# A second modulation's multiply-adds placed in other quanta of one fp32 kernel

## The reference, cut to what matters

```python
for l in range(2):
    mod  = silu(c)     @ w_mod[l] + b_mod[l]       # 2048 -> 6144: shift, scale, gate
    cmod = silu(c_ctx) @ w_mod[l] + b_mod[l]
    h  = rmsnorm(x,  norm_g[l]) * (1 + scale)  + shift
    hc = rmsnorm(cx, norm_g[l]) * (1 + cscale) + cshift
    ...                                            # u = h @ w_in; attention mixers; y * silu(gate part)
    x  = x  + gate  * (y  @ w_o[l])
    cx = cx + cgate * (yc @ w_o[l])                # only l = 0
```

## Time and profile before

| | us |
|---|---|
| median of 3 runs | 2377.14 (2376.76 to 2377.52) |
| the profiled execution, device time | 2377.5 |
| its span in the trace | 2375.7 |
| PE busy | 2330.6 |
| DVE busy | 1502.2 |
| ACT busy | 1040.7 |
| POOL busy | 271.1 |

### The profile page before, as it was taken

One profiled execution on the slowest core, in us unless ns is written; L12 is line 12 of the kernel. 1 busy time (PEld: TensorE's weight loads), 2 busy tenths in 40 slices (PEclk: granted clock), 3 DMA queues, 4 the chain that ended last, 5 costly groups with the idle time before them and its releaser, 6 DMA issues. The chain is left out here.

```text
span 2375.7 us, 31312 instructions
## 1 busy us (share of the span) xinstructions
PE 2330.6 (98%) x11556; PEld 1895.8 (80%) x11556; DVE 1502.2 (63%) x2508; ACT 1040.7 (44%) x1755; POOL 271.1 (11%) x403
## 2 busy tenths in 40 slices
PE   6999999999999999999999999999999999999998
PEld 1578888877778888877878889878888888998887
DVE  2288555666777887877656666675675544544655
ACT  3232333344443222524544455444454445654543
POOL 0011120111110000012121000100110001101200
PEclk9999999999999999999999999999999999999999
DMA  9978454544434756585665556765655676667653
GB/s 369 365 265 282 163 168 138 167 153 160 143 113 166 238 190 224 181 270 190 191 199 156 164 190 202 223 214 162 218 173 187 191 224 196 203 196 239 190 194 135
DMA packets 236423, 474.60 MB, mean 200 GB/s; under 512 B 18886, under 2 KB 47924, under 8 KB 235504
## 3 DMA queue, kind: packets, MB, share of 16 engines
q1 hardware_dynamic: 210768, 394.27, 51.0%
q0 software_dynamic: 25216, 77.81, 10.4%
q10 hardware_dynamic: 288, 0.52, 0.1%
HBM read 438.59 MB, written 33.94 MB: 199 GB/s over the span
## 5 line engine op out<-in xcount | busy, mean ns | idle before, releaser
L2334 PE MATMUL pp<-w_hi,hT_hi 128*128 128x512 f32 (+4 forms) x2520 | 1004.1, 398 | 1.8 <-DVE w_lo L1682 1.8
L2336 PE MATMUL pp<-w_hi,hT_lo 128*128 128x512 f32 (+4 forms) x2520 | 964.9, 383 | 0.0
L1682 DVE TENSOR_TENSOR w_lo<-raw,w_hi 128x1024 fp32r<-128x1024 f32 (+4 forms) x562 | 658.6, 1176 | 481.0 <-ACT w_hi L1379 479.4
L2335 PE MATMUL pp<-w_lo,hT_hi 128*128 128x512 f32 (+4 forms) x2520 | 962.1, 382 | 0.0
L1379 ACT ACTIVATE w_hi<-raw 128x1024 fp32r<-128x1024 f32 (+4 forms) x562 | 569.4, 1018 | 427.3 <-PE pp L2336 300.8
L2334 PEld LDWEIGHTS pp<-w_hi,hT_hi 128*128 128x128 f32 x2520 | 473.9, 188 | 100.5 <-issue 21.4
L2336 PEld LDWEIGHTS pp<-w_hi,hT_lo 128*128 128x128 f32 x2520 | 473.0, 188 | 89.5
L2335 PEld LDWEIGHTS pp<-w_lo,hT_hi 128*128 128x128 f32 x2520 | 474.5, 188 | 80.4 <-issue 4.3
L1792 DVE SCALAR_TENSOR_TENSOR arena<-raw,cT,arena 128x512 f32<-128x512 f32 x240 | 170.4, 745 | 2.1 <-DMA raw<-in_w_mod_dram 0.2
L1549 ACT ACTIVATE arena<-pY 128x512 f32<-128x512 f32 (+2 forms) x122 | 63.5, 520 | 197.9 <-PE pY L2504 192.6
L2329 PE MATMUL pp<-hT_hi,w_hi 128*128 128x512 f32 x352 | 149.6, 425 | 0.0
(11 more groups left out here) (358 smaller groups left out, 2010.7 us busy)
## 6 DMA issues: line engine op xcount, KB each, us to landing
raw<-in_w_in_dram SPq DMA_DIRECT2D x168, 512.0 KB, 4.2
raw<-in_w_mod_dram SPq DMA_DIRECT2D x153, 512.0 KB, 5.4
raw<-in_e_w_in_dram SPq DMA_DIRECT2D x90, 512.0 KB, 5.5
raw<-in_w_o_dram SPq DMA_DIRECT2D x64, 512.0 KB, 4.2
raw<-in_o_w_in_dram SPq DMA_DIRECT2D x64, 512.0 KB, 4.7
raw<-in_w_out_dram SPq DMA_DIRECT2D x64, 512.0 KB, 3.9
raw<-in_w_in_dram SPq DMA_DIRECT2D x56, 440.0 KB, 4.0
arena<-in_w_mod_dram SPq DMA_DIRECT2D x39, 512.0 KB, 11.2
```

The costliest lines, as they stand in the source:

```text
L1682: dve.tensor_tensor(w_lo[:, g.s % SPLIT, 0:n], raw_of(g)[:, 0:n], w_hi[:, g.s % SPLIT, 0:n].bitcast(F32), ALU.subtract).then_inc(lo_done, 1)
L2334: pe.matmul(dst, hT_hi[:, kk, o:o + P], hi[:, k, :], start=a, stop=False)
L2335: pe.matmul(dst, hT_hi[:, kk, o:o + P], lo[:, k, :], start=False, stop=False)
L2336: ins = pe.matmul(dst, hT_lo[:, kk, o:o + P], hi[:, k, :], start=False, stop=z)
```

## The change

Only `Work.room` is edited.

```diff
         if slot < a0:
-            return (slot - b0) % 4 in (0, 2)
+            return (slot - b0) % 4 in (0, 2, 3)
         if slot < C["y0_3"].q0:
-            return (slot - a0) % 4 in (0, 3)
+            p = (slot - C["y0_0"].q0) % 32
+            if slot > C["y0_0"].q0 + 16 and p in (0, 3, 31):
+                return 0
+            return (slot - a0) % 4 in (0, 3) or slot > C["y0_0"].q0 and p in (10, 14, 18)
```

## The result

| | before | after |
|---|---|---|
| median of 6 runs each | 2376.95 us (2375.42 to 2377.59) | 2392.99 us (2391.29 to 2399.15) |
| ratio | | 1.0072, 95% interval 1.0061 to 1.0082 |
| the profiled execution, span | 2377.5, 2375.7 | 2396.15, 2394.3 |
| granted TensorE clock over the span | 0.999 | 0.995 |

The kernel became slower by 16.0 us, outside the range of the forecast (2372.5 to 2386). The profiled execution stands 3.2 us above its median. The spans differ by 18.6 us, and that is what the traces are asked to explain.

A forecast was written before the change was run, and what follows sets the result against it. PE, busy 98% of the span, was taken as the bound, so only its idle time could be gained. -5.39 + 0.9 + 6.5 + 0.5 = +2.5 us gave 2380.0, as a median 2379.6; range 2372.5 to 2386.

The forecast's parts named there:

- (a): Ends of y0_0 and y0_1: PE's idle 0.89 and 1.55 us go; gain 2.44 us.
- (b): scale1_2's second fold waits for the first's reduction; folds move to 468 and 469; gain 0.34 us.
- (c): Head of the c heads: multiply-adds at 668 to 680 go and d_q's loads go out earlier; gain 2.08 us.
- (d): gate1_3's fold waits for bank O; at 660 no head uses the bank; gain 0.53 us.
- The first heads: Three quanta of four there: 33 more multiply-adds on DVE fit its idle time; cost nothing.
- C: Rival: DVE's cover in the first heads is used up, eight units lose about 0.7 each: +5.6, 2385 us; chance 0.06.
- D: Rival: the c heads' chain is one of latencies, so 2.08 of gain goes: 2381.7 us; chance 0.10.
- Quantum 468: Quanta 468 and 469: scale1_2's first fold stands just ahead of y_turn's transpose in bank O; cost 0.9 us (0.5 to 2.5).
- The largest term: Quanta 600 to 624: gate1_1's pair 5 holds its buffer over the gap, loads come late, PE stands 6.5 us (0 to 8).
- rival A: The stall at 624 does not come because buffers come free early enough: 2373.1 us; chance 0.20.
- Rival B: The ring does not recover; longer stall, store chain and 468 cost, or a second ACT wait: about 2386 us; chance 0.14.
- The store chain: c_kv's store and load: fuller queue plus 1.2, POOL's root without the multiply-add minus 0.7; net cost 0.5 us.

The follow-up runs named there:

- hold: The kernel after with all four gate1 chunks back at their places of before (first multiply-add at 597): 2374.97 us.
- straddle: The kernel before with gate1_0 one quantum sooner (596, was 597), so its pair 3 has multiply-adds at 600 and 612: 2393.24 us.
- first: The kernel before with only the first heads' line changed to three quanta in four, so gate1 starts at 581: 2396.43 us.
- keys: The kernel after with one more wait on SP: c_q1's pair 7 is loaded only when the first c head's keys are back: 2389.43 us.
- thin: The kernel after with the loads of gate1_0's and gate1_1's weight pairs cut to 8 of 512 columns: 2387.21 us.
- no600: The kernel after with no multiply-add beside quantum 600, so gate1_1's pair 5 lies wholly behind the gap (612 and 613): 2377.26 us.
- nokeys: The kernel after with gate1_1 from 612, gate1_3 from 684 and scale1_2 from 425, without an added SP wait for the keys: 2371.29 us.
- hold1: The kernel after with only gate1_1 held until quantum 612, gate1_0 staying at 581 to 592: 2374.62 us.

## Why the prediction was wrong

**The gains were right.** -5.39 was forecast. The traces show -2.6 for (a) and -0.85 for (b), for which 2.44 and 0.34 stood. For (c) and (d) 2.61 stood, and PE's idle time at 672 to 720 fell from 3.38 to 0.77, by just that. The quanta there are 4.5 faster because the folds of 676 and 719 went out of them too, some 0.6 each; they were not gained but stand at 644 and 660 now. The first heads cost nothing, as reasoned from the earlier trace rows; hold shows it in the time. Rivals C and D fall.

**Quantum 468:** 0.79 of idle time for the 0.9 forecast, 1.25 in the quanta's times.

**The largest term, 6.5 beside 624:** 6.58. The place, the start of it (one buffer held from 600 to 612), SP's gap and ACT's third wait came as written, and rival A falls. That the length agrees so closely is in part luck, for the chain before it ran otherwise. The term was one stall where the mechanism gives several. The first of ACT's waits, for a load that took 6.8 us and not 3.95, already holds an x_turn activation (2.43); the second holds gate1_1's last multiply-adds and so its fold (1.16). I had followed the chain to the one wait that ended last and not priced those before it. The quanta 608 to 656 cost 12.0 for 6.5.

**The step that failed** is the sentence "Once PE has stood, all other engines are ahead and no further stall follows." They are not ahead: PE stood because ACT and SP were late, and SP's lateness was in the ring, where each load waits for a side pair and each side pair for a load. At 1058.72, 43 us behind the stall, ACT still waited 7.73 us for a load. So quanta 656 to 672 cost 6.95 where the sum had 0.5. Of the kernels with the pair across the gap straddle pays 4.9 there, first 3.7, keys 3.0 and thin 2.8; no600, without it, pays 1.9. That a stall follows is shown; its size in after is not explained. Rival B had this in its condition (a second ACT wait) and stopped at 2386 with 0.14; it was the nearest to the truth, and still 7 us short.

That sentence is one of three parts of the error. The spans moved by 18.6 us for a forecast of 2.5, 16.1 too much: 6.5 at 656 to 672, 5.5 at 608 to 656 (above), 6.1 at 592 to 608, which had no term (below), and 0.35 at 468, less 2.6 by which the gains and the folds that moved away came to more.

**The store chain, 0.5 (0 to 3):** 4.59 of stall for 1.30, and 3.0 of slow clock. I had asked whether the queue would be fuller, and not whether ACT would bring the evictions late. keys shows the queue's share; no600, whose store waits 7.99 us and whose stalls there are 0.73 and 1.61, suggests that the state of the ring comes first. The minus 0.7 for POOL's root was wrong as well. It still takes 1.93 us, and the low half alone stands beside it (kernel after, POOL and DVE):

```profile
1083.78 1.93 POOL L1303 TENSOR_TENSOR stat<-stat 128x4 f32<-128x4 f32 x1 [5.60 <-DVE stat L1972]
```
```profile
1083.60 1.22 DVE L1685 TENSOR_TENSOR w_lo<-raw,w_hi 128x1024 fp32r<-128x1024 f32 x1
```

I had put the longer root down to the multiply-add, which was gone here. The two roots that I compared also have different shapes, 128x4 and 128x2. Compared at one shape, POOL's root still differs with what DVE does beside it: 128x2 took 0.71 us in the kernel before at 1068.26, where DVE started a low half 0.4 us into it, and 1.59 in nokeys at 1062.11, where one ran beside two thirds of it.

The Trainium skill (DMA: Bandwidth & Descriptors, Queues, rings and completion order) says that a DMA engine goes round between the queues that have work. The traces agree: POOL stood 9.77 us beside the row of loads and 6.00 with a load held.

**A place not looked at:** quanta 581 to 608. The table of the change has gate1_0 at 581 to 592 and gate1_1 from 593, at up to two multiply-adds per quantum, and the working begins at 600. Their loads share the ring and the DMA engines with out0_3's last pairs, just where the norm's chain begins, which x_turn needs at once. 6.1 us, 2.9 of it slow clock. The forecast had no term for them.

**The clock.** A stall was priced at its length. Three of them brought 7.6 us more.

As terms, from the earlier trace rows on: stalls 3.21 + 2.43 + 1.16 + 6.58 + 0.76 + 3.83 - 1.30 = 16.7; slow clock 7.6; 468 1.25; gate1_3's fold, now at 660, 0.6; and -2.6, -0.85 and -4.5. The sum is 18.2 for the 18.6 measured.

## What to carry to other kernels

When work is moved through a ring of buffers, look first for an item whose uses lie on both sides of a gap: its buffer holds the queue for the whole gap (25 us here). Moving the pair's first multiply-add to the other side, with those behind it one place on, was worth 16 us. After such a hold don't close the account at the first stall: follow the ring until it is again a lap ahead, price each wait of the in-order engine on the way, and add to every stall what the clock takes behind it. And walk through every stretch where the new table has work and the old had none, not only those where a rule changes.

## What the hardware showed that I had not expected

- PE idle of 3.21, 6.58 and 3.83 us (after) was each followed or overlapped by 6.8 us at 1.2 GHz. Idle of 1.75 (no600), 2.33 (hold1) and 2.43 (after) was not, but 2.25 in thin and 2.13 in keys were followed by 3.4 us each. So a stall of 2 to 3 us may cost its length alone or some 1.7 us more. Its length does not decide it: 4.12 (keys, at quantum 606) and 4.70 (straddle) had 3.4 us behind them, and 2.94 (straddle) had 6.8.
- Making gate1_0's and gate1_1's loads nearly empty did not shorten the stall at 624: 6.48 for 6.58 us. The other loads of the chain were whole.
- From POOL's issue of the second c_kv store to that of the keys' load: 3.7 us in nokeys, 6.7 in keys, 8.8 before, 10.5 after, for the same store each time, with other loads of SP around it.
